# Six score levels, two transposes and the state update of the gated linear attention placed half a weight unit later

## What is computed

```python
def gla_chunk(S, q, k, v, log_f):
    L = q.shape[1]
    idx = jnp.arange(L)
    b = jnp.cumsum(log_f, axis=1)
    mask = (idx[:, None] >= idx[None, :])[None, :, :, None, None]
    diff = b[:, :, None] - b[:, None, :]
    w = jnp.where(mask, jnp.exp(jnp.where(mask, diff, 0.0)), 0.0)
    scores = jnp.sum(q[:, :, None] * k[:, None, :] * w, axis=-1)
    intra = jnp.einsum('btsh,bshv->bthv', scores, v)
    inter = jnp.einsum('bthd,bhdv->bthv', q * jnp.exp(b), S)
    b_last = b[:, -1]
    S_new = (jnp.exp(b_last)[..., None] * S
             + jnp.einsum('bshd,bshv->bhdv', k * jnp.exp(b_last[:, None] - b), v))
    return S_new, intra + inter
```

## Time and profile before

| | us |
|---|---|
| median of 3 runs | 1419.89 |
| lowest and highest run | 1417.8, 1420.12 |
| the profiled execution | 1420.84 |
| its span in the trace | 1419.0 |
| PE busy | 1386.3 |
| DVE busy | 776.7 |
| ACT busy | 521.3 |
| POOL busy | 147.1 |

### The profile page before, as it was taken

How to read it: one execution, slowest core, us unless ns; L and a number is a source line. 1 busy time by engine, 2 the same in 40 slices (tenths; PEclk the granted TensorE clock), 3 DMA queues, 4 the chain that set the end, 5 groups by cost and what they waited for, 6 DMA issues and landing times. The chain is left out here.

```text
span 1419.0 us, 28637 instructions
## 1 busy us (share of the span) xinstructions
PE 1386.3 (98%) x12590; PEld 1344.8 (95%) x12590; DVE 776.7 (55%) x1224; ACT 521.3 (37%) x859; POOL 147.1 (10%) x107
## 2 busy tenths in 40 slices
PE   8999999999999999999999999999999999999996
PEld 8899898899999999999998998989999999999996
DVE  6897767745434334344768967675453343433433
ACT  5333556633223223123433345565331231322331
POOL 0200000031110110200202000001301102002012
PEclk9999999999999999999999999999999999999997
DMA  6113333222222222222221224422222222222211
GB/s 230 61 65 100 95 118 95 78 102 90 88 81 87 89 90 90 90 90 89 77 75 46 67 88 132 134 74 77 88 90 90 90 90 90 85 82 88 89 61 63
DMA packets 50635, 127.82 MB, mean 90 GB/s; under 512 B 8400, under 2 KB 17744, under 8 KB 50512
## 3 DMA queue, kind: packets, MB, share of 16 engines
q1 hardware_dynamic: 50224, 125.44, 26.7%
q10 hardware_dynamic: 288, 0.55, 0.1%
HBM read 118.77 MB, written 7.21 MB: 89 GB/s over the span
## 5 line engine op out<-in xcount | busy, mean ns | idle before, releaser
L1302 PE MATMUL PS<-xhi,whi 128*128 128x272 f32 x1920 | 565.0, 294 | 4.0 <-DVE wlo L767 3.1
L1302 PE MATMUL PS<-xhi,wlo 128*128 128x272 f32 x1920 | 557.2, 290 | 0.0
L1302 PE MATMUL PS<-xlo,whi 128*128 128x272 f32 x1920 | 554.8, 289 | 0.0
L767 DVE TENSOR_TENSOR wlo<-raw,whi 128x1024 fp32r<-128x1024 f32 x200 | 252.9, 1264 | 386.1 <-ACT whi L467 385.3
L467 ACT ACTIVATE whi<-raw 128x1024 fp32r<-128x1024 f32 x200 | 211.5, 1059 | 548.4 <-PE PS L1302 543.9
L1302 PEld LDWEIGHTS PS<-xhi,whi 128*128 128x128 f32 x1920 | 363.2, 189 | 15.5 <-issue 9.7
L1302 PE MATMUL PS<-zhi,wlo 128*128 128x272 f32 x1280 | 371.0, 290 | 0.0
L1302 PE MATMUL PS<-zhi,whi 128*128 128x272 f32 x1280 | 368.8, 288 | 0.4 <-DVE wlo L767 0.4
L1302 PE MATMUL PS<-zlo,whi 128*128 128x272 f32 x1280 | 368.7, 288 | 0.0
L1302 PEld LDWEIGHTS PS<-xlo,whi 128*128 128x128 f32 x1920 | 363.8, 189 | 0.2
L1302 PEld LDWEIGHTS PS<-xhi,wlo 128*128 128x128 f32 x1920 | 363.3, 189 | 0.0
(11 more groups left out here) (226 smaller groups left out, 1050.3 us busy)
## 6 DMA issues: line engine op xcount, KB each, us to landing
raw<-in_wu SPq DMA_DIRECT2D x199, 512.0 KB, 3.4
Bh<-in_bias SPq DMA_DIRECT2D x16, 256.0 KB, 4.1
h<-in_x SPq DMA_DIRECT2D x8, 272.0 KB, 6.1
out_k_t<-att_k SPq DMA_DIRECT2D x8, 272.0 KB, 4.4
out_y_t<-y SPq DMA_DIRECT2D x8, 272.0 KB, 2.7
kct<-in_ck SPq DMA_DIRECT2D x8, 256.0 KB, 3.1
cvb<-in_cv SPq DMA_DIRECT2D x8, 256.0 KB, 4.7
out_v_p<-vtk SPq DMA_DIRECT2D x8, 256.0 KB, 2.2
```

Source lines behind the costliest of these rows:

```text
L767: nc.vector.tensor_tensor(wlo[n % SPL][:, :], raw[n % RAW][:, :], f32(whi[n % SPL][:, :]), ALU.subtract).then_inc(sems["w_lo"], 1)
L1302: return nc.tensor.matmul(out, lhsT, rhs, start=start, stop=stop, skip_group_check=True)
```

## The change

Nine entries of PE_STEPS are moved to the next slot, and DVE_STEPS and ACT_STEPS take them over since they are built from it. ROTARY, the weight steps and everything from `out GLA` on stay where they are.

```diff
     (5, 0): [("diag", GLA)],
-    (5, 1): [("level", 0)], (6, 0): [("level", 1)], (6, 1): [("level", 2)],
-    (7, 0): [("level", 3)], (7, 1): [("level", 4)], (8, 0): [("level", 5)],
-    (8, 1): [("tok", GLA, "v")], (9, 0): [("tok", GLA, "k")], (9, 1): [("kv", GLA)],
+    (6, 0): [("level", 0)], (6, 1): [("level", 1)], (7, 0): [("level", 2)],
+    (7, 1): [("level", 3)], (8, 0): [("level", 4)], (8, 1): [("level", 5)],
+    (9, 0): [("tok", GLA, "v")], (9, 1): [("tok", GLA, "k")], (10, 0): [("kv", GLA)],
     (10, 1): [("out", GLA)], (11, 0): [("out_s", GLA)],
```

## The result

| | before | after |
|---|---|---|
| median of 9 runs, us | 1419.89 | 1424.41 |
| lowest run, us | 1417.8 | 1422.25 |
| the profiled execution, us | 1420.84 | 1424.16 |
| its span, us | 1419.0 | 1422.4 |

The ratio after to before is 1.0031, 95% interval 1.0020 to 1.0042: the change makes the kernel slower by some 4.4 us. One of the nine runs of after took 2698.03 us and is in the slower state: it does not enter the ratio, and the other eight lie between 1422.25 and 1425.25 with a median of 1424.29. Three of the eight took 1422.25 to 1422.69 and five 1424.16 to 1425.25; the profiled execution is one of the five. The prediction of 1422.0 had the direction and the size too small; 1424.41 lies 0.21 above the range's upper end.

What follows compares the result with a forecast made beforehand. PE was taken as the bound, with DVE second in the changed stretch. Two layers' waits +0.6, a lost fall -1.3 and new falls +2.8 gave +2.1 us: 1422.0 against the median 1419.89, range 1418.8 to 1424.2.

Steps and rivals of the forecast that it cites:

- What bounds the kernel: Whole kernel: PE busy 98% of the span; DVE a second bound in the stretch that the change touches.
- Step 1: Ahead of level 0: PE's wait goes, a gain of 1.83 us in layer 0 and 1.82 in layer 1.
- Step 2: Ahead of the transpose of gv: a wait of about 3.0 us (2.8 to 3.2) where it was 0.65.
- The collision: DVE steps beside POOL's products ahead of level 5's masked copy: two of 2.03 and 2.12 us, a third product adds 0.4.
- Step 3: Behind the transpose of gv: new wait of 0.4 to 0.6 us at `out`; layer ends 0.3 later, two layers +0.6.
- Step 4: Clock: the fall behind level 0 in layer 1 goes, -1.3; falls behind both new waits come, +2.8; in all +1.5 us.
- Rival 2: Masked copy of level 5 later than 87.0, all three POOL products holding up DVE by 1.4; 1424.0, chance 0.19.
- Rivals 1 and 3: One or neither new wait brings a fall, 1420.6 or 1419.2, 0.27; collisions fall away and no fall comes, 1416.8, 0.04.

Runs made afterwards that it cites:

- the filled kernel: The change with 24 unread matmuls put ahead of the transpose of gv, over PE's wait there; 1418.97 us, ratio to before 0.9995.
- the first 5 filled one: First trace of the change with 5 unread matmuls put ahead of the transpose of gv; median 1421.48 us, traced execution 1419.67.

## Why the prediction was wrong

- **What bounds the kernel: right.** DVE is the second bound in this stretch. The runs show it from both sides: moved rotary work moved the waits and left 2.98 of 3.74 us of them, and lighter DVE steps took most of the long wait away.
- **Step 1: right.** No stop ahead of level 0 in either layer.
- **Step 2: right.** 3.16 and 3.15 us, forecast 2.8 to 3.2, from the cause named: the kernel with ROTARY moved along has 0.24.
- **The collision: right in kind, and in sum.** The three POOL products held up DVE steps by 0.9, 1.4 and 0.6, where I had 1.3, 1.4 and 0.4. With POOL's product cut the steps took their usual 0.72. The Trainium skill, page "SBUF — State Buffer", section "Who interferes with whom", has this as an exclusive hold. The traces agree: each held DVE step ended 0.58 us after POOL's product.
- **Step 3: right.** 0.58 us at `out`, forecast 0.4 to 0.6; without the slow stretch the layer ends 2.88 - 2.56 = 0.32 later, forecast 0.3.
- **Step 4: the term that failed is the price of a fall, "1.4 each: +2.8".** The falls came behind both waits, as I took it. Their price was taken from the one fall whose two layers could be compared, 1.3 to 1.47, after a wait of 1.82, with the clock low for 3.4 us. Behind 3.16 us it is 2.56 to 2.63, in four of four, with the clock low for 6.8 us. So the term is +5.1, and 2.3 us were missing. I took one sample as the price of every fall and gave it no upper bound in the range.
- **The sum with that term mended: 2.1 + 2.3 = 4.4, and partly luck.** On the median it gives 1419.89 + 4.4 = 1424.3, against 1424.41. On the profiled execution it gives 1420.84 + 4.4 = 1425.2, against 1424.16: the fall behind the back transposes, -1.14, had no term. The prediction had taken 0.95 off between the two, for a reason that no run separates. And the median of before was 1419.3 in all later measurements.
- **The rivals.** Rival 2 gave 1424.0, nearly the time, by a mechanism that did not happen: the masked copy ended at 86.8, not beyond 87.4. Rivals 1 and 3 did not come; that a missing fall brings the time down was shown in the filled kernel.
- **The range.** Executions of one kernel spread over 3 to 4 us. The falls behind its short waits and at the start, 1.1 to 1.3 us each, come in one trace and not in the next and would give such a spread; that they do is argued, not shown. A term that is paid or not is a spread of the measured time too, and the upper side should have held a dearer fall.

## What to carry to other kernels

When work is placed by hand for each engine, move everything that its consumers stand behind: here a side table kept four short steps in their old slot, and 2.9 us of DVE work came ahead of the copy that PE waits for. Cut the waits of a busy TensorE into pieces or put unread matmuls over them: waits of 1.7 to 1.8 us were followed by a fall in 2 of 10 cases, at 1.3 us where it could be priced, and waits of 3.2 us in 4 of 4, at 2.6 us more in slow matmuls. And do not carry the price of one fall over to another: after equal waits it was 2.8 and 1.4 us, so keep its range open upwards. Read the start of a trace too: a fall there moves the whole execution by 1.3 us whatever was changed behind it.

## What the runs showed of the hardware beyond that

- The granted clock fell about 2 us into the long wait, while PE was still idle, and stayed at 1.2 GHz for 5.6 us of work after its end. After the wait of 6.1 us it was 6.1 us of work in one layer and 2.8 in the other.
- Waits of 1.1 us, the same two in nearly every kernel, were followed by a fall in some executions and not in others, 4 of 26 cases in all: in one of two layers of before, in both of the kernel with `kv` alone moved, in none of the two traces of the change. What sets it was not found. The Trainium skill, page "TensorE: Matmul & The Clock Gate", section "Why this matters for your kernels", warns of longer gaps only; these traces differ from it.
- Behind PE's wait for the first wlo (1.3 to 2.9 us, ended at about 9 us) the clock fell in 11 of 13 traces and stayed up in two, the first 5 filled one and before with level 0's wait filled, whose diagonal scores start 1.3 us earlier than those of before.
